# Two value groups and four pairs of the output projection placed between the attention heads, and every other weight low made on POOL

## The reference

```
h    = modulate(rms_norm(x, pre_mix_g), shift1, scale1)
proj = h @ w_in                                   # pooling channels | q latent | kv latent | rope key
y_pool = multiscale_pool(proj[..., :1024], w_pool, pool_scale)
y_mla  = mla_attention(...)                       # 8 heads: scores, softmax, p @ v
y    = concat([y_pool, y_mla]) @ w_out            # the output projection, 2048 x 2048
x    = x + gate1 * rms_norm(y, post_mix_g)
h    = modulate(rms_norm(x, pre_ffn_g), shift2, scale2)
y    = peer_ffn(h, w_q, sub_keys, expert_u, expert_v)   # 16384 experts, top 16 of each of 8 heads
x    = x + gate2 * rms_norm(y, post_ffn_g)
```

## Time and profile before

| what | us |
|---|---|
| median of three runs | 2076.1 |
| the profiled execution, its own time | 2077.25 |
| its span | 2075.3 |
| PE busy in the span | 1905.2 (92%) |
| DVE busy | 1492.3 (72%) |
| ACT busy | 948.2 (46%) |
| POOL busy | 658.6 (32%) |
| chain that ended last, share of PE | 85% |

### The profile page before, as it was taken

One profiled execution on the slowest core, in us unless ns is written; L12 is line 12 of the kernel. 1 busy time (PEld: TensorE's weight loads), 2 busy tenths in 40 slices (PEclk: granted clock), 3 DMA queues, 4 the chain that ended last, 5 costly groups with the idle time before them and its releaser, 6 DMA issues.

```text
span 2075.3 us, 33816 instructions
## 1 busy us (share of the span) xinstructions
PE 1905.2 (92%) x10307; PEld 1627.5 (78%) x10307; DVE 1492.3 (72%) x2053; ACT 948.2 (46%) x1498; POOL 658.6 (32%) x347
## 2 busy tenths in 40 slices
PE   0489989899999999999999997689999999999997
PEld 0479758799788888888888886578887888788886
DVE  6998679763888889998887668967675555455555
ACT  1043344443444444445554448854444444444443
POOL 1000020000888888889974446600000000000000
PEclk9789969899999999999999999999999999999999
DMA  9989569990666666666677762057766666665554
GB/s 390 415 306 384 201 254 385 287 219 19 164 187 186 185 187 185 185 187 175 184 191 189 189 159 91 0 184 286 288 233 183 203 204 207 234 210 194 192 193 151
DMA packets 229619, 439.10 MB, mean 212 GB/s; under 512 B 23538, under 2 KB 158144, under 8 KB 216000
## 3 DMA queue, kind: packets, MB, share of 16 engines
q1 hardware_dynamic: 225648, 416.31, 63.5%
q0 software_dynamic: 3888, 22.14, 3.0%
q10 hardware_dynamic: 32, 0.01, 0.0%
HBM read 434.12 MB, written 4.21 MB: 211 GB/s over the span
## 4 chain that ended last, share of the span: by engine, by line
PE 85%; DVE 6%; issue 4%; DMA 2%; ACT 1%; POOL 1%; SPq 1%; DVEq 0%; ACTq 0%; POOLq 0%
PE ps L883 21%; PE ps L885 11%; PE ps L933 11%; PE ps L934 11%; PE ps L936 11%; PE ps L655 4%; PE ps L657 4%; PE ps L656 4%; PE ps L916 3%; DVE acc L1338 3%; PE ps L650 2%; DMA raw<-in_peer_v_dram 1%; DMA i<-consts_dram 1%; POOL eL L546 1%; PE ps L644 1%
## 5 line engine op out<-in xcount | busy, mean ns | idle before, releaser
L883 PE MATMUL ps<-h,eH 128*128 128x512 f32 x2048 | 722.0, 397 | 5.7 <-POOL eL L546 5.6
L546 POOL TENSOR_TENSOR eL<-raw,eH 128x1024 fp32r<-128x1024 f32 x224 | 552.1, 2471 | 291.8 <-ACT eH L1192 291.6
L885 PE MATMUL ps<-h,eL 128*128 128x256 f32 x2048 | 574.8, 281 | 0.0
L1795 DVE TENSOR_TENSOR eL<-raw,eH 128x1024 fp32r<-128x1024 f32 x256 | 313.2, 1225 | 300.3 <-ACT eH L1285 300.2
L883 PEld LDWEIGHTS ps<-h,eH 128*128 128x128 f32 x2048 | 385.0, 188 | 100.3 <-POOL eL L546 8.0
L1285 ACT CAST eH<-raw 128x1024 fp32r<-128x1024 f32 x256 | 269.8, 1054 | 390.4 <-PE ps L936 336.5
L1192 ACT CAST eH<-raw 128x1024 fp32r<-128x1024 f32 x256 | 269.3, 1052 | 366.2 <-PE ps L885 303.0
L933 PE MATMUL ps<-eH,aH 128*128 128x512 f32 x1024 | 400.4, 391 | 7.3 <-DVE eL L1795 7.3
L934 PE MATMUL ps<-eL,aH 128*128 128x512 f32 x1024 | 400.0, 391 | 0.0
L1714 DVE STREAM_TRANSPOSE raw<-raw 128x1024 f32<-128x1024 f32 x256 | 317.2, 1242 | 104.7 <-DMA raw<-in_peer_u_dram 97.7
L885 PEld LDWEIGHTS ps<-h,eL 128*128 128x128 f32 x2048 | 387.4, 189 | 0.0
(11 more groups left out here) (270 smaller groups left out, 2360.0 us busy)
## 6 DMA issues: line engine op xcount, KB each, us to landing
raw<-in_peer_u_dram SPq DMA_DIRECT2D x1024, 128.0 KB, 2.9
raw<-in_peer_v_dram SPq DMA_DIRECT2D x256, 512.0 KB, 3.7
ring<-in_ada_w_dram SPq DMA_DIRECT2D x40, 2048.0 KB, 18.7
ring<-in_w_out_dram SPq DMA_DIRECT2D x8, 2048.0 KB, 16.1
ring<-in_peer_wq_dram SPq DMA_DIRECT2D x32, 512.0 KB, 19.4
piece<-in_ada_w_dram POOLq DMA_DIRECT2D x13, 1024.0 KB, 5.7
ring<-in_w_in_dram SPq DMA_DIRECT2D x6, 2048.0 KB, 14.9
ring<-in_w_uq_dram SPq DMA_DIRECT2D x2, 1536.0 KB, 9.0
```

The source lines that it names most:

```text
L546: pool.tensor_tensor(by_k(eL[:, j % RING, :]), turned(raw[:, j % RAW, :]), by_k(eH[:, j % RING, :].bitcast(F32)), ALU.subtract).then_inc(u ...
L883: pe.matmul(ps[:, bank, :], eH[:, slot, k * P:(k + 1) * P], h2[:, kk].rearrange("p a t -> p (a t)"), start=kk == 0, stop=False, skip_group ...
L885: mm = pe.matmul(ps[:, bank, 0:T], eL[:, slot, k * P:(k + 1) * P], h2H[:, kk, :], start=False, stop=kk == KT - 1, skip_group_check=True)
L1795: dve.tensor_tensor(eL[:, slot, :], raw[:, slot, :], eH[:, slot, :].bitcast(F32), ALU.subtract).then_inc(v_lo, 1)
```

## The change

- Only scores 0 and 1 and value groups 0 and 1 stand before the first head (with scores 2 behind them); groups 2 and 3 stand behind heads 0 and 1. Scores use two banks of PSUM instead of three. `load_order` and `released` are as they were.
- Pairs 0 to 3 of column chunk 0 stand behind heads 3, 4, 6 and 7 on PE, their casts in the same turns on ACT (into two buffers of their own, `early_high`), their lows behind the normalising of these heads on DVE.
- Of the other 28 pairs POOL makes the lows with odd j, 14 in all, behind the row it reads back; DVE makes the even ones. They are counted apart (`w_lo_pool`).
- Shift 2 and scale 2 are made on DVE behind the diagonals, not ahead of the sums of squares; the banks of the x1 turns are in another order so that the last two are those that hold the column sums. The second wq low comes one step later.
- In the scatter ACT makes the distances of a group and then the Relus of the group before.

```diff
-X1_BANK = (2, 3, 0, 1, 4, 5, 6, 7)
+X1_BANK = (2, 3, 4, 5, 6, 7, 0, 1)
...
+    early_high = [at(f"early_high{i}", M + 8192 + 1024 * i, [1024], F32R) for i in range(2)]
...
+        EARLY_PAIRS = 4
+
+        def pool_makes(kind, n, j):
+            return kind == "wout" and j % 2 == 1 and (n > 0 or j >= EARLY_PAIRS)
+
+        low_count = {}
+        made = {True: 0, False: 0}
+        for kind in ("win", "wout", "wq"):
+            for n in WEIGHTS[kind][0]:
+                for j in range(8):
+                    by_pool = pool_makes(kind, n, j)
+                    made[by_pool] += 1
+                    low_count[(kind, n, j)] = made[by_pool]
+
+        def wait_weight_low(eng, kind, n, j):
+            eng.wait_ge(w_lo_pool if pool_makes(kind, n, j) else w_lo, low_count[(kind, n, j)])
+
         def released(key):
...
+            at_ = order.index(n) * 8 + j
+            if kind == "wout":
+                if at_ < EARLY_PAIRS:
+                    return early_high[at_ % 2][:, 0:2 * cols].rearrange("p (k n) -> p k n", k=2)
...
-        S_BANK = (4, 5, 0)
+        S_BANK = (4, 5)
+        OUT_BANK = ((0, 1), (6, 7), (4, 5), (6, 7))
+        PAIR_HEAD = (3, 4, 6, 7)
+        V_BANK = (2, 6, 0, 1)
...
+            for n in range(4):
+                for j in range(8):
+                    if pool_makes("wout", n, j):
+                        pool.wait_ge(w_hi, pair_no("wout", n, j) + 1)
+                        ks = slice((2 * j) % 8, (2 * j) % 8 + 2)
+                        pool.tensor_tensor(wide_low("wout", n, 2 * j)[:, ks, :], wide("wout", n, 2 * j)[:, ks, :],
+                                           high_of("wout", n, j).bitcast(F32), ALU.subtract).then_inc(w_lo_pool, 1)
...
-                b = S_BANK[h % 3]
-                if h >= 3:
-                    pe.wait_ge(s_max, h - 2)
+                b = S_BANK[h % 2]
+                if h >= 2:
+                    pe.wait_ge(s_max, h - 1)
...
-            for h in range(3):
+            for h in range(2):
...
+            def values(m):
+                hh, tt = m // 2, m % 2
+                mm_group(ps[:, V_BANK[m], :], lambda k: cT[:, 4 + k, tt * P:(tt + 1) * P],
+                         lambda k: wkv[:, k, 4 * hh:4 * hh + 4, NOPE:2 * NOPE], 2).then_inc(v_mm, 1)
+
+            for m in range(2):
+                pe.wait_ge(pool_out, 4 * m + 2)
+                values(m)
+
+            def out_pair(n, pair):
+                wait_weight_low(pe, "wout", n, pair)
...
-                        if n >= 2 and k == 0:
-                            pe.wait_ge(y_out, (n - 2) * 2 + tt + 1)
-                        mm = split3(ps[:, 4 + (n % 2) * 2 + tt, :], cat_high(k)[:, tt * P:(tt + 1) * P],
+                        if n == 3 and k == 0:
...
+                mm.then_inc(w_used, 1)
+
+            scores(2)
+            pe.wait_ge(v_out, 2)
+            pe.wait_ge(pool_out, 8)
+            pe.wait_ge(gcol_ready, 1)
+            for h in range(HEADS):
+                if h == 3:
+                    pe.wait_ge(v_out, 4)
+                turn_probs(h)
+                if h + 3 < HEADS:
+                    scores(h + 3)
+                mix(h)
+                if h < 2:
+                    values(2 + h)
+                if h in PAIR_HEAD:
+                    out_pair(0, PAIR_HEAD.index(h))
+            pe.wait_ge(o_out, HEADS - 1)
+            gate_rows(0, 2)
+
+            for n in range(4):
+                if n == 1:
+                    pe.wait_ge(pT_out, HEADS)
+                for pair in range(8):
+                    if n or pair >= EARLY_PAIRS:
+                        out_pair(n, pair)
...
+                if k == 12:
+                    pe.wait_ge(mod2_ready, 2)
...
+                if kind == "wout" and n == 0 and 2 <= j < EARLY_PAIRS:
+                    act.wait_ge(w_used, pair_no(kind, n, j) - 1)
...
+            def values_out(m):
+                act.wait_ge(v_mm, m + 1)
+                act.copy(vv[:, m % 2, (m // 2) * W:(m // 2 + 1) * W], ps[:, V_BANK[m], :]).then_inc(v_out, 1)
...
-                if h == 1:
-                    values_out()
+                    values_out(0)
+                    values_out(1)
                 if h == HEADS:
-                    weight_high("wout", 0, 0)
+                    weight_high("wout", 0, EARLY_PAIRS)
                 if h >= 2:
                     outs(h - 2)
+                if h in (2, 3):
+                    values_out(h)
+                if h in PAIR_HEAD:
+                    weight_high("wout", 0, PAIR_HEAD.index(h))
...
+            def distances(g, q, first):
...
+            def gated_hots(g, q):
...
-                    hot_first(r * 4 + q, q, False)
+                    distances(r * 4 + q, q, False)
+                    gated_hots(r * 4 + (q - 1), (q + 3) % 4)
+            gated_hots(T // 4 - 1, 3)
...
+                    if k == 0 and i == 4:
+                        dve.wait_ge(w_used, pair_no("wout", 0, 2 + h) + 1)
...
-                if h == 4:
+                if h == 1:
                     gate_column(0, 2, 1, V_B2, V_PO1)
+                if h - 2 in PAIR_HEAD:
+                    weight_low("wout", 0, PAIR_HEAD.index(h - 2))
...
-                    weight_low("wout", n, j)
+                    if (n or j >= EARLY_PAIRS) and not pool_makes("wout", n, j):
+                        weight_low("wout", n, j)
...
-            shift_column(mod2[:, 1, :], 3, 0, V_B3)
-            dve.nop().then_inc(mod2_ready, 1)
-            scale_column(mod2[:, 0, :], 4, 1, V_B4, V_G2)
-            dve.nop().then_inc(mod2_ready, 1)
...
+            shift_column(mod2[:, 1, :], 3, 0, V_B3)
+            dve.nop().then_inc(mod2_ready, 1)
+            scale_column(mod2[:, 0, :], 4, 1, V_B4, V_G2)
+            dve.nop().then_inc(mod2_ready, 1)
...
-                if j in (0, 2, 4, 6):
-                    weight_low("wq", 0, 1 + j // 2)
+                if j in (1, 2, 4, 6):
+                    weight_low("wq", 0, (0, 1, 2, 0, 3, 0, 4)[j])
```

More of the change, by code:

```diff
@@ L274, in hybrid_block @@
         w_hi, w_lo, w_used, cat_hi, cat_lo = sem("w_hi"), sem("w_lo"), sem("w_used"), sem("cat_hi"), sem("cat_lo")
+        w_lo_pool = sem("w_lo_pool")
         raw_in = [sem(f"raw_in{s}") for s in range(RAW)]
@@ L342, in high_of @@
             cols = cols_of(kind, n)
-            return bufs[(order.index(n) * 8 + j) % len(bufs)][:, 0:2 * cols].rearrange("p (k n) -> p k n", k=2)
+            at_ = order.index(n) * 8 + j
+            if kind == "wout":
+                if at_ < EARLY_PAIRS:
+                    return early_high[at_ % 2][:, 0:2 * cols].rearrange("p (k n) -> p k n", k=2)
+                at_ -= EARLY_PAIRS
+            return bufs[at_ % len(bufs)][:, 0:2 * cols].rearrange("p (k n) -> p k n", k=2)
         def weight_parts(kind, n, k):
@@ L679, in _ @@
                     if k % 2 == 0:
-                        pe.wait_ge(w_lo, pair_no("win", n, k // 2) + 1)
+                        wait_weight_low(pe, "win", n, k // 2)
                     wh, wl = weight_parts("win", n, k)
@@ L785, in mix @@
                           skip_group_check=True).then_inc(o_mm, 1)
-            for h in range(3):
+            for h in range(2):
                 scores(h)
             pooled(3)
[L790 to L808, removed]
+            def values(m):
[7 more added lines that the diff above has]
+                wait_weight_low(pe, "wout", n, pair)
+                for k in (2 * pair, 2 * pair + 1):
                     if n == 0 and k >= 8:
@@ L850, in _ @@
                     if k % 2 == 0:
-                        pe.wait_ge(w_lo, pair_no("wq", n, k // 2) + 1)
+                        wait_weight_low(pe, "wq", n, k // 2)
                     wh, wl = weight_parts("wq", n, k)
@@ L1127, in y_squares @@
                 for tt in range(TT):
-                    b = 4 + (n % 2) * 2 + tt
+                    b = OUT_BANK[n][tt]
                     act.activation(y1[:, tt, n * W:(n + 1) * W], ps[:, b, :], ACT.Square,
@@ L1133, in _ @@
                 for j in range(8):
-                    if n or j >= 1:
+                    if n or j > EARLY_PAIRS:
                         weight_high("wout", n, j)
-                    if n == 0 and j == 3:
-                        gate_out(0, 1)
+                    if n == 0 and j == 5:
+                        gate_out(0, 2)
                     if n and j == 2:
@@ L1247, in _ @@
             gelu(TILES - 2, 0)
-            def hot_first(g, q, first):
+            def distances(g, q, first):
                 if not first:
@@ L1263, in _ @@
             act.wait_ge(gate_minus, 1)
-            hot_first(0, 0, True)
+            distances(0, 0, True)
+            gated_hots(0, 0)
             gelu(TILES - 1, 1)
-            for q in range(1, 4):
-                hot_first(q, q, True)
+            distances(1, 1, True)
+            for q in range(2, 4):
+                distances(q, q, True)
+                gated_hots(q - 1, q - 1)
             with act.Fori(1, T // 16) as r:
```

(8 more changed lines are left out.)

4 lines of the change are left out of this document (2 added, 2 removed).

## The result

The changed kernel takes 2084.4 us in the median of 9 runs, the kernel before 2076.3 of 9 on the same chip: ratio 1.0048, 95% interval [1.0029, 1.0066]. In a second set it was 1.0053 [1.0035, 1.0071]. By the medians it is slower by 8.1 and 11.9 us; 2088.3 was predicted, 11.1 more than the kernel before.

What follows compares the result with a forecast made beforehand. In the output projection it took PE as never idle and VectorE as equally full, and ScalarE as pacing the scatter. 9.5 + 3 + 10 - 3.4 - 8.0 = +11.1 on 2077.25 gave 2088.3 us, range 2068 to 2098.

Steps and rivals of the forecast that it cites:

- The heads' part: Attention heads up to the fifth pair: late load less the four hidden pairs, net +9.5 us.
- the part from the fifth pair on: Last 28 projection pairs: 3 us at POOL's first lows plus 10 us from POOL's lows holding VectorE.
- the scatter's gain: Scatter of the gates: closing ScalarE's idle gap in each looped group saves 8.0 us.
- Step 1: Values between heads: head 0 turns at about 254.3 instead of 256.2; fourth value group ends at 266, not 255.4.
- Step 2: SyncE's queue: wout's first half lands at 286, ScalarE stands from 266.5, mix of head 2 comes 15.6 us late.
- Step 3: Mix of head 2 to fifth pair: 32.7 us instead of 39.5, clock returning in the first pair; net +9.5 us.
- rival (c): Heads: the clock stays at 0.50 from head 3 to pair 4, +18 for +9.5, 2097 us; chance 0.11.
- Step 4: Last 28 pairs: waits at POOL's first lows +3 us; POOL's lows hold VectorE up to 2.2 each, +10.
- Step 5: Turn to x1: shift and scale run beside the turns, PE goes on earlier; -3.4 us, bounds 0 and 4.
- Step 6: Scatter: ScalarE sets the pace, looped groups go from 1.63 to 1.50 apart; -8.0 us, bounds 0 and 8.5.
- Rival (b): Heads: wout's wait costs nothing or is recovered, so the early pairs pay off; 2053 to 2065 us, chance 0.13.
- Rival (d): Scatter: the groups keep their idle 0.17 us, +8, 2096 us; chance 0.05.

Runs made afterwards that it cites:

- e2: The changed kernel with all four value groups ahead of head 0 again; ratio 0.9985 [0.9968, 1.0001] to the kernel before.
- e1: The changed kernel with all lows of the output projection made by VectorE again; ratio 1.0007 [0.9989, 1.0026] to the kernel before.
- e5: The changed kernel run again, unedited; 2085.58 us against 2073.72 for the kernel before, ratio 1.0053.
- e9: The changed kernel with POOL making 7 of the last 28 lows instead of 14; fifth pair to last matmul 86.8 us in one execution.
- e4: The kernel before with only shift and scale of the second norm behind diag, plus the bank order and later wq low; ratio 0.9985 [0.9971, 1.0].
- e3: The kernel before with only the scatter edit, next group's distances between the halves of a group; ratio 0.9934 [0.991, 0.9958].
- e6: The changed kernel with all value groups ahead of head 0 and all lows on VectorE; ratio 0.9932 [0.9909, 0.9955] to the kernel before.
- e7: As e6, but with the four early pairs behind heads 4 to 7; ratio 0.9948 [0.993, 0.9966] to the kernel before.
- e8: The kernel before with the scatter and x1 edits together, nothing else; 2058.76 us, ratio 0.9928 [0.9901, 0.9954].

## Why the prediction came out as it did

The forecast (2088.3, slower) was right, and both costs that it named are there: e2 takes away the late load, e1 POOL's lows. Its sizes were less good than its sum. The heads' part was 3.7 us too small, the part from the fifth pair on 3 too large, and the scatter's gain 4 too small; the first two cancelled each other, which is luck.

- **Step 1**: head 0 turned at 254.70 (predicted 254.3). The fourth value group ended at 270.2, not 266. The granted clock went down while PE was idle for 2.68 us ahead of head 0 (0.81 in the window 252 to 254, 0.50 from 254), where it had held until 260 before. So head 0 with the third group ran at the lower level and took 8.95 us instead of the 5.1 of the prediction (the group alone 3.42 instead of 1.76); head 1 with the fourth took 6.5, as predicted.
- **Step 2**: the landing came 18.4 behind the group (19.7), ScalarE stood 17.80 (19.5), the mix of head 2 was at 290.96 (288.3). e2 shows it by taking it away.
- **Step 3**: mix 2 to fifth pair 34.4 us (32.7). The clock came back 2.7 us into the first pair, as forecast; rival (c) falls. Up to the start of the fifth pair the prediction had +9.5; measured +13.2, and +15.7 in e5. It had no term for the fifth pair's own low, which stands behind VectorE's five sums: 3.66 us of PE's wait (2.08 in e5), and without it these heads took less than the 32.7.
- **Step 4**: 3 for the first lows and 10 for the rest make 13; measured from the fifth pair on were +10.05 in the profile, 9.8 against e1, and +10.8 in e5. The 3 was a wait for POOL's first low: the first profile does not have it, e5 has it with 3.87. The holding of each low was "up to 2.2", in the mean 1.85 in one profile and 1.6 in the other. That the 10 was met is partly luck: in e9 PE's loss does not go down in step with the number of lows, as my sum over eight pairs would have it, and the sum had no term for the granted clock behind PE's waits.
- **Step 5**: -3.4 predicted, -3.34 measured; e4 -3.1.
- **Step 6, the mis-sized term**: -8.0 predicted, -11.9 measured (e3: -11.8 in the trace). I took the pace of the groups written out, 1.50, for ScalarE's own. But there the second half of a group still stood directly behind its first. With another group's distances in between, ScalarE issues a distance pair in 0.59 and the second pair in 0.77 to 0.9, so that at its quickest it needs 0.59 + 0.77 = 1.36 for a group. The groups come 1.425 apart, and VectorE, busy for all of it, has 2.85 for two: it sets the pace now. The bound of 8.5 was wrong: it was the gap, not a bound of the engine behind.
- **Rival (b)**, that the pairs are worth 12: e6, e7 and e8 show no gain from them even with hardly any wait for the load. What the trace shows beside that: from the turn of head 0 to the fifth pair PE was idle for 8.9 us before and for 10.2 in e6, so on balance the pairs filled no idle time; VectorE is full from 300 us on (12.78 of 13.00 in e6), and the fifth pair waits 3.66 for its low; and head 0 turned at 259.23 in e6, 256.22 before, as the scores of head 2, with two score banks, stand behind the values and VectorE's normalising of head 0 behind their maxima. None of these was tried alone. **Rival (d)** falls with e3.
- By the anchors, terms of 23.3, -3.3 and -11.9 stand against the forecast's 22.5, -3.4 and -8.0: +8.1 for +11.1.

## What to carry to other kernels

Before work is given to a second engine to relieve a full one, look for a row in which both run at once: if the two hold each other, the help costs more than it takes off (here 1.6 to 1.85 us of holding for 1.22 us saved). Count with it the lower clock that can follow a wait of TensorE, as in e9. A load early in a shared queue is as late as the wait in front of it, so a step that frees its slot must not be moved behind work that needs the load. And when a gap on the pacing engine is closed, its new bound is its own issue pace in the new order and the next engine's load, not the pace of the old order without the gap.

## What the runs showed of the chip that was not expected

One stage, one code, two paces. Windows of PE in the first expert stage, the kernel before, then e2, then e5 (length, busy PE, matmuls, granted clock, DMA share, GB/s); the clock granted is 1.00 in all:

```profile
600.00:700.00 100.00, 100.00 (x568) 1.00 0.67 186
1100.00:1200.00 100.00, 100.00 (x579) 1.00 0.74 189
```
```profile
600.00:700.00 100.00, 100.00 (x579) 1.00 0.67 189
1100.00:1200.00 100.00, 100.00 (x579) 1.00 0.72 189
```
```profile
600.00:700.00 100.00, 100.00 (x568) 1.00 0.65 186
1100.00:1200.00 100.00, 100.00 (x568) 1.00 0.72 184
```

PE is never idle and does 568 or 579 matmuls in 100 us. An execution can change from one pace to the other. Over the stage of some 725 us that makes up to 14 us (an estimate, 725 x 11/579); the anchors have 720.7 (e2, the quicker pace in both windows) to 730.9 (e5, the slower in both), and the runs of the kernel before in these sets lie from 2065.9 to 2081.7. So one pair of profiles could not tell this change's sign with safety, and the stretches that it touches, read apart, could. What sets the pace stays open.

VectorE's held operations are not only those with two tiles as inputs, which the prediction had in mind. Its normalising of head 2 (two instructions, of 128 and 256 columns, each with one tile and a column as inputs; the view prints both under the first shape) took 3.91 us from 267.75, beside POOL's 2048-column low, and 0.67 to 1.12 for the other heads. It delayed nothing that the sum rests on, since the fourth value group was through at 270.2. The two steps of L1405 in e5 (one tile and a column too, 5.6 instead of 1.4) are a second case:

```profile
266.31 5.20 POOL L553 TENSOR_TENSOR catL<-catT,catH_a 128x2048 fp32r<-128x2048 f32 x2 [4.06 <-ACT catH_a L1182]
```
```profile
267.75 3.91 DVE L1602 TENSOR_SCALAR s_sb<-s_sb,stat 128x128 f32<-128x128 f32 x2
```
